# Outer products of a sample state on two row groups in the order 0, 2, 1, 3, state stores waited for head by head, and chunk products ahead of two gate projections

## The reference, cut to what matters

```
def gla_sample(q, k, v, la, state):            # for each of 8 sample tokens and 4 heads
    st = exp(lat)[..., None] * st + kt[..., :, None] * vt[..., None, :]
    o  = einsum('bhd,bhdv->bhv', qt, st)
def gla_prompt(q, k, v, la):                   # 4 chunks of 64 tokens
    kv = einsum('nbhsd,nbhsv->nbhdv', k_out, vc)          # one product for each chunk and head
    st = d_c[..., None] * st + kv_c                       # scan over the chunks
    o  = intra + einsum('nbhtd,nbhdv->nbhtv', q_in, s_prev)
...
o_g = rmsnorm(o_g, g_gla) * silu(gg)           # gg: the output gate, part of the input projection
```

## Time and profile before

| | us |
|---|---|
| median of 3 runs | 1509.52 (1507.57 to 1510.23) |
| the profiled execution, its own time | 1503.03 |
| its span from first to last instruction | 1501.0 |
| PE busy | 1422.1 (95% of the span) |
| DVE busy / ACT busy / POOL busy | 383.1 / 254.9 / 83.6 |
| mean granted clock of PE | 0.983 of full speed |

### The profile page before, as it was taken

How to read it: one execution, slowest core, us unless ns; L and a number is a source line. 1 busy time by engine, 2 the same in 40 slices (tenths; PEclk the granted TensorE clock), 3 DMA queues, 4 the chain that set the end, 5 groups by cost and what they waited for, 6 DMA issues and landing times.

```text
span 1501.0 us, 19360 instructions
## 1 busy us (share of the span) xinstructions
PE 1422.1 (95%) x8023; PEld 770.2 (51%) x8023; DVE 383.1 (26%) x940; ACT 254.9 (17%) x551; POOL 83.6 (6%) x104
## 2 busy tenths in 40 slices
PE   7988999899999889999999999999999999999997
PEld 5745887668888663443443343443443443442433
DVE  2643333220123351221221221221231231121222
ACT  3322332231112320110110110101011011010102
POOL 1441211100101000000000000000000000000000
PEclk9999999999999979999999999999999999999999
DMA  9574454743555658999999999999899999999993
GB/s 341 187 239 141 150 174 153 236 158 112 187 206 225 234 225 341 398 425 428 430 427 428 430 427 427 431 428 391 368 427 431 427 427 430 428 427 429 429 427 158
DMA packets 62440, 494.83 MB, mean 330 GB/s; under 512 B 5263, under 2 KB 6472, under 8 KB 37816
## 3 DMA queue, kind: packets, MB, share of 16 engines
q1 hardware_dynamic: 50904, 453.98, 73.1%
q0 software_dynamic: 11488, 40.15, 8.2%
HBM read 487.07 MB, written 7.05 MB: 329 GB/s over the span
## 4 chain that ended last, share of the span: by engine, by line
PE 82%; DMA 12%; DVE 3%; issue 1%; ACT 1%; SPq 0%; DVEq 0%; ACTq 0%
PE bank L1145 23%; PE bank L655 16%; PE bank L1172 13%; DMA ring<-in_w_gate_up 6%; DMA arena<-in_w_down 6%; PE bank L1128 5%; PE bank L614 4%; PE bank L1184 4%; PE bank L1131 2%; PE bank L770 2%; PE bank L1152 2%; PE bank L627 2%; PE bank L679 1%; PE bank L1158 1%; PE bank L910 1%
## 5 line engine op out<-in xcount | busy, mean ns | idle before, releaser
L1145 PE MATMUL bank<-ring,arena 128*64 128x512 f32 x1536 | 345.5, 599 | 5.2 <-DMA ring<-in_w_gate_up 5.2
L1172 PE MATMUL bank<-arena 128*64 128x512 f32 x976 | 217.2, 595 | 8.9 <-DMA arena<-in_w_down 8.9
L1145 PEld LDWEIGHTS bank<-ring,arena 128*64 128x64 f32 x1536 | 104.7, 137 | 224.8 <-issue 211.9
L655 PE MATMUL bank<-arena,ring 128*128 128x264 f32 x896 | 206.9, 391 | 0.0
L655 PEld LDWEIGHTS bank<-arena,ring 128*128 128x128 f32 x896 | 169.7, 192 | 32.1 <-issue 3.5
L2155 DVE TENSOR_TENSOR resid<-resid,bank 128x264 f32<-128x264 f32 x128 | 54.9, 429 | 340.5 <-PE bank L1184 339.0
L1172 PEld LDWEIGHTS bank<-arena 128*64 128x64 f32 x976 | 67.8, 137 | 143.3 <-issue 124.5
L1145 PE MATMUL bank<-arena 128*64 128x512 f32 x512 | 115.3, 592 | 0.0
L2160 DVE TENSOR_SCALAR arena<-bank 128x512 f32<-128x512 f32 x32 | 22.0, 687 | 307.2 <-PE bank L1145 307.2
L1128 PE MATMUL bank<-arena 128*128 128x128 f32 x544 | 82.4, 297 | 10.7 <-DVE resid L2155 8.5
L1128 PEld LDWEIGHTS bank<-arena 128*128 128x128 f32 x544 | 69.1, 199 | 23.8 <-DVE resid L2155 13.1
(11 more groups left out here) (299 smaller groups left out, 1119.0 us busy)
## 6 DMA issues: line engine op xcount, KB each, us to landing
ring<-in_w_gate_up SPq DMA_DIRECT2D x96, 2048.0 KB, 22.8
arena<-in_w_down SPq DMA_DIRECT2D x61, 2048.0 KB, 18.8
arena<-in_w_gate_up SPq DMA_DIRECT2D x32, 2048.0 KB, 26.8
ring<-in_w_in SPq DMA_DIRECT2D x10, 2048.0 KB, 9.0
ring<-in_w_down SPq DMA_DIRECT2D x3, 2048.0 KB, 41.4
out<-arena POOLq DMA_DIRECT2D x10, 512.0 KB, 5.2
arena<-in_state_gla POOLq DMA_DIRECT2D x8, 512.0 KB, 4.7
ring<-in_w_o_mla SPq DMA_DIRECT2D x2, 2048.0 KB, 8.1
```

Of the source, the lines that this page charges most:

```text
L655: mm = nc.tensor.matmul(lin_bank(name)[0:m, 0:width], w(ring_name, nk, cols)[:, k, a:a + m], rhs[:, k, 0:width], start=(k == 0), stop=(k = ...
L1145: mm = nc.tensor.matmul(B[i // 2][CAP * (i % 2):CAP * (i % 2) + CAP, :], xg[:, k, CAP * e:CAP * e + CAP], slot(n)[:, a:a + 512], start=Fal ...
L1172: mm = nc.tensor.matmul(B[4][CAP * half:CAP * half + CAP, :], hT[:, c, CAP * (k // 4):CAP * (k // 4) + CAP], slot(j)[:, a:a + 512], start= ...
```

## The change

The sample keys and values of heads 0 and 1 now stand on partitions 0 to 7, those of heads 2 and 3 on partitions 32 to 39, and PE takes the heads in the order 0, 2, 1, 3. So `ks` is copied out of PSUM in two parts of 256 columns rather than in one of 512; `ks_tok` is cleared first, and a mask of the identity summed over its four 32-row blocks, `row_mask`, takes the place of the identity's column. The 8 multiplications run over 64 partitions and 256 columns rather than over 8 and 512. The chunk products of head 3 go behind gg6, and gg7 is last; ACT waits for the two stores of `st_buf[h]` just ahead of head h, where it waited for all eight at once, and takes gg6 out ahead of kv6. DVE scans head by head, each as soon as its two products are copied out, with a wait for the instruction before it at every step.

```diff
-       + [f"kv{n}" for n in range(8)] + ["gg6", "gg7", "spick"]
+       + [f"kv{n}" for n in range(6)] + ["gg6", "kv6", "kv7", "gg7", "spick"]
...
-        vs_tok, ks_tok = A[64:72, A_SMALL + 256:A_SMALL + 1280], A[64:72, 14816:15328]
-        k_rows = slot(3)[64:72, :].rearrange("p (b n) -> p b n", b=SAMPLE)
+        vs_tok, ks_tok, row_mask = view(A_SMALL + 256, 512), A[0:64, 14816:15072], view(15072, 32)
+        k_rows = slot(3)[0:64, 0:2048].rearrange("p (b n) -> p b n", b=SAMPLE)
+        def row_parts(name):
+            if name == "ks":
+                return [(ks_tok[32 * g:32 * g + SAMPLE, :], SAMPLE, (256 * g, 256 * g + 256)) for g in range(2)]
...
-                for h in range(H_GLA):
-                    mm = nc.tensor.matmul(B[5 + h // 2][:, DV * (h % 2):DV * (h % 2) + DV], k_rows[:, b, 128 * h:128 * h + 128],
-                                          vs_tok[:, DV * h:DV * h + DV], start=True, stop=True)
+                for h in (0, 2, 1, 3):
+                    rows, i = slice(32 * (h // 2), 32 * (h // 2) + SAMPLE), h % 2
+                    mm = nc.tensor.matmul(B[5 + h // 2][:, DV * i:DV * i + DV], k_rows[rows, b, 128 * i:128 * i + 128],
+                                          vs_tok[rows, DV * i:DV * i + DV], start=True, stop=True)
...
             for h in range(H_GLA):
+                if h == 3:
+                    project(["gg6"], "gg1", 8, 512, n_T, first=256)
                 for odd in range(2):
                     open_bank(f"kv{2 * h + odd}")
...
-            project(["gg6", "gg7"], "gg1", 8, 512, n_T, first=256)
+            project(["gg7"], "gg1", 8, 512, n_T, first=384)
...
-            for i in range(4):
-                act.wait_ge(S(f"state_out{i}"), 32)
             for n in range(8):
                 h, odd = n // 2, n % 2
+                if n == 6:
+                    out("gg6", silu_gg[:, 6, :], ACT.Silu)
+                if odd == 0:
+                    act.wait_ge(S(f"state_out{h}"), 32)
                 out(f"kv{n}", states[:, h, odd:4:2, :], src=lin_bank(f"kv{n}")[:].rearrange("p (c v) -> p c v", c=2))
-            for c in (6, 7):
-                out(f"gg{c}", silu_gg[:, c, :], ACT.Silu)
+            out("gg7", silu_gg[:, 7, :], ACT.Silu)
...
+                if u == 10:
+                    V.memset(ks_tok, 0.0)
+                    link(V.tensor_reduce(row_mask, ident.rearrange("p (j e) -> p e j", j=4), AX, ALU.add))
...
-                        V.tensor_scalar(k_rows[:, b, :], ks_tok, ident[64:72, 64 + b:65 + b], None, ALU.mult).then_inc(S("k_rows"), 1)
+                        V.tensor_scalar(k_rows[:, b, :], ks_tok, row_mask[0:64, b:b + 1], None, ALU.mult).then_inc(S("k_rows"), 1)
...
-            lin_done(dve, "kv7")
-            for c in range(1, NCH):
-                for h in range(4):
+            for h in range(4):
+                lin_done(dve, f"kv{2 * h + 1}")
+                for c in range(1, NCH):
                     ins = V.scalar_tensor_tensor(out=states[:, h, c, :], in0=states[:, h, c - 1, :], scalar=ge[:, h, CH * c + CH - 1:CH * c + CH],
                                                  in1=states[:, h, c, :], op0=ALU.mult, op1=ALU.add)
-                if c < NCH - 1:
-                    link(ins)
+                    if h < 3 or c < NCH - 1:
+                        link(ins)
```

More of the change, by code:

```diff
@@ L325, in build @@
         AT = xview(3072, 512).rearrange("p (c h t) -> p c h t", c=2, h=H_GLA)
-        vs_tok, ks_tok = A[64:72, A_SMALL + 256:A_SMALL + 1280], A[64:72, 14816:15328]
-        k_rows = slot(3)[64:72, :].rearrange("p (b n) -> p b n", b=SAMPLE)
+        vs_tok, ks_tok, row_mask = view(A_SMALL + 256, 512), A[0:64, 14816:15072], view(15072, 32)
[3 more added lines that the diff above has]
+                return [(ks_tok[32 * g:32 * g + SAMPLE, :], SAMPLE, (256 * g, 256 * g + 256)) for g in range(2)]
+            n = int(name[1])
+            c, g = n // 2, n % 2
+            if n < 4:
+                return [(v_tok[:, c, 512 * g:512 * g + 512], P, (0, 512))]
+            return [(vs_tok[32 * g:32 * g + SAMPLE, :], SAMPLE, (0, 512))]
         o_tok = view(12608, 2048, D)
@@ L1425, in rows_of_unit @@
                     if TI[name] % 2:
[L1426 to L1432, removed]
+                        turn_out(name, row_parts(name))
             def unit_exp(h):
```

## The result

The changed kernel takes 1494.41 us (median of 5 runs, 1493.21 to 1499.79), the kernel before 1508.85 (1507.57 to 1510.23, 5 runs): ratio 0.9911, interval 0.9891 to 0.9931. The profiled execution is the median one: 1494.41, span 1492.6, beside 1503.03 and 1501.0 of before. So the two profiled executions differ by 8.6, the medians by 14.4; much of what follows is about that gap.

A forecast was written before the change was run, and what follows sets the result against it. The prediction took PE as the bound up to the experts and transfers among them, counting savings one to one. 6.7 + 1.7 + 1.8 = 10.2 us off the median 1509.5 gave 1499.3, range 1496.3 to 1504.5.

The forecast's parts named there:

- The term of the stores: ACT's copies ahead of the chunk products: waiting only for tokens 0 and 4 starts them 2.05 earlier; net 1.8 us.
- The outer products: Sample loop on PE: each token's group falls from 1.93 to 1.09 on two row groups, eight times; 6.7 us.
- the row with 64 rows: Profile row for one head of chunk products, 8 passes in 1.09 us, taken as model for the 8-row outer products.
- the alternation: Those chunk products switch between two row groups at every matmul; the forecast of 1.09 a group leaned on this.
- no overlap: Rival in the outer products: 8-row products don't overlap, the change on PE does nothing; gain 1.8, 1507.7 us; chance 5%.
- slower: Rival in the outer products: each change between row groups costs 0.33; 6.1 us slower, 1515.6; chance 3%.
- What is costed at nothing: Clearing ks_tok, the mask, the 8 multiplications and SP's zm0 loads: hidden or shifting along, 0 us.
- what is late next: Head 3's scan stays hidden with about 1 us to spare, token 7's state load with 1.1.
- the rival of heads 1 and 2 waiting for their stores: At the chunk products, the stores of tokens 5 and 6 hold things up; 1.8 goes to 0, 1501.1 us; chance 10%.
- The clock, 1.7: Sample loop: the one projection of six at the low clock, 5.44 instead of 3.76, returns to full speed; 1.7 us.
- The second low stretch: 283 to 290 us, clock 0.51, behind tokens 6 and 7's waits for DVE: expected to stay; up to 3.1 more if gone.
- The shift from the median: Whole run: the summed 10.2 us taken from the median 1509.5, which lies 6.5 above the profiled execution; 1499.3 us.

The follow-up runs named there:

- order_0123: The changed kernel with the heads in natural order 0, 1, 2, 3, still on two row groups: 1496.59 us, ratio 0.9908 to the kernel before.
- batch_scan: The changed kernel with DVE's scan as before, 12 steps in a row behind all eight copies: 1500.12 us, ratio 0.9939 to the kernel before.
- rows_only: The kernel before with only the outer products on two row groups and the new head order; chunk products, store waits and scan as before: 1499.44 us, ratio 0.9931.
- chunks_only: The kernel before with only the new chunk product order, head-by-head store waits and scan; outer products on one row group: 1506.27 us, ratio 0.9979.
- twice: The changed kernel with every outer product made twice, 16 passes a group on two row groups: 1504.31 us, ratio 0.9972 to the kernel before.

## Why the prediction was right or wrong

The forecast fell short by 4.2 us. Two steps of it failed. The term of the stores was bounded by 1.8 and measured 3.6; and a shift added up from one execution was set off against the median, whose distance from that execution lies in part where the change acts (the mean piece of six traces is 1.5 longer than the one I read). Of the 4.2 the stores' term makes 1.8 and the outer products 0.3; the rest belongs to the second step, and its cause is in part open. The terms one by one:

**The outer products, 6.7.** Right. 8 x (1.93 - 1.06) = 7.0; the row with 64 rows was a good one for 8 rows. The reason in it was half wrong: I leaned on the alternation, and order_0123 does as well without. The rivals "no overlap" and "slower" are out with the 1.06.

**What is costed at nothing, and what is late next.** Right: the scan ends 1.0 ahead of gg7's end, and batch_scan shows 2.28 of waiting without it; the load for token 7 is hidden; the rival of heads 1 and 2 waiting for their stores didn't come, the four copies run from 284.36 as one row of 2.06 with no wait.

**The wait for the stores, 1.8.** The mechanism was right, the size wrong. In traces the term is 68.67 - 65.12 = 3.6 (the means of rows_only and after; their medians on one chip differ by 5.1, with intervals that overlap). Besides the 1.8 it holds the low clock behind the wait, 1.6, which this kernel has in five of six traces, and not in the one I read. The prediction's "0 to 1.8" as bounds of this term was the faulty step: the wait on PE had a second price behind it, and I weighed the clock only where the one trace showed a fall. With the outer products on one row group the same edit measured less, 3.3 between medians (0.6 to 5.7), and 1.9 between the mean pieces, where the second trace of chunks_only had two slow projections; so the size of the term is less sure than its direction.

**The clock, 1.7.** Right in outcome: the slow projections are gone in every trace with two row groups, and the mean of before is 1.0 a loop. As single loops had 0 to 3 of them, it was luck that the one I read had the mean number. The reason given, that the groups get shorter, isn't shown, and twice speaks against it; what ended the falls stays open. The second low stretch stayed, as forecast, though it was shorter in the profiled execution (0.66 over 5.00 us, where it was 0.51 over 7.00). The traces of after with a clock of 0.97 over the piece are 0.5 to 0.9 us shorter than those with 0.95, so of the bound of 3.1 more at most that much came.

**The shift from the median.** Here the sum lost most. The terms were read from an execution of 1503.03, with a higher mean clock than most (0.983), and set off against a median 6.5 higher, "for reasons that the trace does not show". Part of those reasons lies in what the change takes away. The mean granted clock has a median of 0.977 in 42 runs of before (the two largest groups) and 0.981 in 22 runs of after; as the low level is half of the full one, that is 2 x 0.023 x 1509 = 69 us at the low level against 2 x 0.019 x 1494 = 57. In the 42 runs the span falls and rises with this time, 0.3 to 0.4 us for each us (correlation 0.9): 12 us less of it are 4 to 5 us of span. With 7.0 and 1.8 it makes 12.8 to 13.8. This is an estimate, and a rough one: over all runs of before on record the median clock is 0.978, which makes 12 us into 9.6 and the sum 12.0 to 12.6.

What is accounted for: 11.6 in the traces' pieces (7.0 outer products, 1.7 slow projections, 3.6 stores with their low stretch, together 12.3, which is 0.7 too much). The medians of the pairs differ by 14.4, 15.3, 13.2 and 12.7; by the intervals of their ratios the gain is at least 10.4, 12.7, 9.5 and 8.8, so only one pair shows more than 11.6 beyond its noise. The remaining 1.1 to 3.6 us are not placed. Outside the piece the traces of one chip show no gain. On the chip with the 13.2 the traces themselves differ by 12.8, so little is missing there. On the chip with the 15.3, the traced execution of before was 1.8 under the median of before and that of after 1.7 above its own, and their pieces differ by 11.8. So the traced executions did not have all that the median ones had; whether that is further falls of the clock is argued, not shown.

## What to carry to other kernels

Small products whose weights sit on few partitions were worth spreading over two row groups even without interleaving them: a pass of 256 columns cost 0.216 us on one and 0.109 on two, and each change of tile shape around the group still cost 0.33 of weight-load wait. A wait of PE costs more than its length when the clock is low behind it (1.6 behind the stores, 1.5 behind the scan of batch_scan), so price the removal of a wait with the pieces behind it at both levels (2.12 and 2.96 here). Read more than one execution before setting terms against a median: if the profiled one is some us off, the difference may belong to the very effects that the change touches.

## What was not expected of the hardware

The same loop of the same program had 0 to 3 slow projections of 5.44 in different executions, with pieces from 75.29 to 80.45. The order of neighbours on two row groups made no difference: 1.06 and 1.07. Groups of 16 passes on two row groups (1.93) had no slow projection behind them in the one trace of twice (clock 1.00 from 236 to 276 us), while 8 passes on one row group, also 1.93, came with one or more in five of eight traces. Why is open.
